# A two-block decoder kernel: key weights of the second memory attention taken out of the weight ring, four of its eight key tiles computed in four earlier openings

## The reference, cut to what matters

```python
def second_block(x, mem, ...):
    mem_n = rms_norm_2(mem, mem_norm)                 # 256 memory tokens, once for both layers
    for i in range(2):
        g = ln_gains[i]
        hn = rms_norm_2(x, g[0])
        t = rglru_mixer(hn, ...) if i == 0 else rwkv7_mixer(hn, ...)
        x = x + rms_norm_2(t, g[1])
        c = mem_cross_attention(rms_norm_2(x, g[2]), mem_n, c_w_q[i], c_w_kv[i], c_w_o[i])
        x = x + rms_norm_2(c, g[3])
        m = sqrelu_mlp(rms_norm_2(x, g[4]), m_w_up[i], m_w_down[i])
        x = x + rms_norm_2(m, g[5])
```

## Time and profile before

| | |
|---|---|
| median of 3 runs | 3470.85 us (3470.57 to 3474.96) |
| the profiled execution's own time | 3472.6 us |
| span in the profile | 3470.8 us |
| mean granted TensorE clock | 0.999 |
| PE busy | 3429.4 us, 99% of the span |
| PEld, DVE, ACT, POOL busy | 77%, 48%, 41%, 40% |
| DMA | 317.43 MB, mean 91 GB/s |
| L1053, products of memory keys | 256 records, 56.5 us |
| L593, fillers | 72 records, 34.7 us |

### The profile page before, as it was taken

The page is one execution under the profiler, slowest core; times in us unless marked ns, Lnnn a source line. Parts: engine busy times, 40 slices in busy tenths (PEclk is TensorE's granted clock), DMA queues, the critical chain, the costliest instruction groups (busy, mean ns, idle before and its releaser), DMA issues.

```text
span 3470.8 us, 52494 instructions
## 1 busy us (share of the span) xinstructions
PE 3429.4 (99%) x19196; PEld 2686.1 (77%) x19196; DVE 1652.4 (48%) x2657; ACT 1416.0 (41%) x2843; POOL 1387.3 (40%) x1112
## 2 busy tenths in 40 slices
PE   9999999999999999999999999999999999999999
PEld 7877787888788777888887777788874677868887
DVE  2565666442335765764424643412257874433032
ACT  3245534332333554343325643533317244444232
POOL 4632244444455223544444152444410222424444
PEclk9999999999999999999999999999999999999999
DMA  4421122222224111222232331222233221213222
GB/s 146 126 86 55 55 79 97 97 97 100 99 96 136 55 55 64 95 91 97 97 103 100 107 103 61 92 97 97 97 133 98 86 64 57 97 55 109 97 97 85
DMA packets 105274, 317.43 MB, mean 91 GB/s; under 512 B 27008, under 2 KB 31232, under 8 KB 104192
## 3 DMA queue, kind: packets, MB, share of 16 engines
q1 hardware_dynamic: 93168, 301.00, 25.8%
q10 hardware_dynamic: 11920, 13.85, 1.5%
HBM read 304.32 MB, written 7.34 MB: 90 GB/s over the span
## 4 chain that ended last, share of the span: by engine, by line
PE 91%; DVE 4%; ACT 1%; DMA 1%; DVEq 1%; issue 1%; SPq 0%; POOL 0%; ACTq 0%; POOLq 0%
PE ps L586 24%; PE ps L588 23%; PE ps L587 23%; PE ps L1338 2%; PE ps L1053 2%; PE ps L775 2%; PE ps L627 1%; PE ps L622 1%; PE ps L795 1%; DMA ring<-in_weights 1%; PE ps L820 1%; PE ps L623 1%; PE ps L1123 1%; PE ps L1157 1%; PE ps L1284 1%
## 5 line engine op out<-in xcount | busy, mean ns | idle before, releaser
L3302 POOL TENSOR_TENSOR ring_r<-ring,rounded_r 128x512 fp32r<-128x512 f32 x505 | 666.9, 1321 | 1803.6 <-ACT rounded_r L1617 1795.2
L586 PE MATMUL ps<-source_hi,rounded_r 128*128 128x512 f32 x2360 | 935.7, 396 | 3.9 <-DVE Y_lo L3237 1.9
L587 PE MATMUL ps<-source_hi,ring_r 128*128 128x512 f32 x2360 | 919.0, 389 | 0.0
L1617 ACT ACTIVATE rounded_r<-ring 128x512 fp32r<-128x512 f32 x512 | 323.1, 631 | 1306.2 <-PE ps L588 1142.8
L3304 POOL TENSOR_TENSOR ring_r<-ring,rounded_r 128x512 fp32r<-128x512 f32 x505 | 704.2, 1394 | 0.0
L588 PE MATMUL ps<-X_lo,rounded_r 128*128 128x512 f32 x1456 | 568.1, 390 | 0.0
L586 PEld LDWEIGHTS ps<-source_hi,rounded_r 128*128 128x128 f32 x2360 | 443.3, 188 | 104.8 <-issue 11.0
L587 PEld LDWEIGHTS ps<-source_hi,ring_r 128*128 128x128 f32 x2360 | 443.6, 188 | 89.1 <-issue 1.9
L588 PEld LDWEIGHTS ps<-X_lo,rounded_r 128*128 128x128 f32 x1456 | 273.2, 188 | 58.0
L1618 ACT ACTIVATE rounded_r<-ring 128x512 fp32r<-128x512 f32 x512 | 316.3, 618 | 0.0
L588 PE MATMUL ps<-N_lo,rounded_r 128*128 128x512 f32 x760 | 296.0, 389 | 0.0
(11 more groups left out here) (534 smaller groups left out, 5509.7 us busy)
## 6 DMA issues: line engine op xcount, KB each, us to landing
ring<-in_weights SPq DMA_DIRECT2D x556, 512.0 KB, 3.3
X<-in_x SPq DMA_DIRECT2D x4, 512.0 KB, 6.8
PAIR<-Z ACTq DMA_DIRECT2D x32, 64.0 KB
residual<-X ACTq DMA_DIRECT2D x1, 2048.0 KB, 9.4
X<-residual SPq DMA_DIRECT2D x1, 2048.0 KB, 9.1
ring<-in_weights SPq DMA_DIRECT2D x16, 128.0 KB, 2.6
SWAP<-Z ACTq DMA_DIRECT2D x4, 256.0 KB, 6.0
MEM<-in_mem ACTq DMA_DIRECT2D x1, 1024.0 KB, 4.9
```

What stands on the lines that cost most here:

```text
L586: mm(o, lh, rh, start=start, stop=False)
L587: mm(o, ll, rh, start=False, stop=False)
L1617: av(RH[:, j, FRONT], ring[:, j, FRONT], ACT.Copy).then_inc(w_hi_half, 1)
L3302: nc.gpsimd.tensor_tensor(RL[:, j, FRONT], ring[:, j, FRONT], RH[:, j, FRONT].bitcast(F32), ALU.subtract).then_inc(w_lo_half, 1)
```

## The change

- The weights of layer 1's memory keys leave `weights` and become an input of their own, `keys`. Two DMAs on ACT's queue bring them into `MIXED` (`KEYS_W`), four tiles each, 2 MB: the first right behind the load of the memory at the start of the second block, the second in the second half of the MLP of `tail(0)`, behind its `up`.
- Key tiles 0 to 3 (`HELD` = 4) are computed ahead of four openings: tile 0 ahead of `lru_out`, in place of `warm(3, 3)`; tile 1 ahead of the queries, in place of `warm(0, 2)`; tile 2 ahead of the product with the values, in place of `warm(4, 2)`; tile 3 around the norm ahead of the MLP, four matmuls ahead of its sums, two ahead of its spread, two behind it, in place of `warm(1, 1)` and `warm(3, 3)`, with `warm(4, 2)` after them.
- ACT copies each of these tiles out of its bank (`key_held`) into the place of its weights. TensorE waits for these copies ahead of lane 3 of two first quads, ahead of the output product, and behind the first quad of `up`. DVE scales the four at the start of its second half of the MLP, and ACT saves them to `D3`.
- Tile 4 takes the place of the first of the eight behind the last `down`. Tiles 5 to 7 follow, and the sums of squares of the norm ahead of RWKV are spread among them: squares 0 and 1, 2 and 3, then 4 to 7.

```diff
-B_RWKV = B_K1 + C_MK
+B_RWKV = B_K1
...
+            def next_keys(c, bank, first=0, end=KT):
+
+                pe.wait_ge(keys_in, KEYS_LANDED + c // HELD * 16 + 16)
+                half = c % 2 if c >= HELD else 0
+                for k in range(first, end):
+                    ins = mm(ps[:, bank, half * S2:half * S2 + S2], KEYS_W[:, c % HELD, k * P:k * P + P], MN[:, k, :], start=(k == 0), stop=(k == KT - 1))
+                if end == KT:
+                    ins.then_inc(keys_made, 1)
...
-                warm(0, 2)
+                if l == 0:
+                    next_keys(1, HELD_BANK[1])
+                else:
+                    warm(0, 2)
...
-                warm(4, 2)
+                if l == 0:
+                    next_keys(2, HELD_BANK[2])
+                else:
+                    warm(4, 2)
...
+                if l == 0:
+                    pe.wait_ge(keys_held, HELD_AT + 3)
                 gemm(B + B_MO, C_MO, AH, YL, t_ready, l * 32 + 8, SRC[f"o{l}"], 4)
+                if l == 0:
+                    next_keys(3, HELD_BANK[3], 0, 4)
                 rms_out(4 + 6 * l)
-                warm(1, 1)
+                if l == 0:
+                    next_keys(3, HELD_BANK[3], 4, 6)
+                else:
+                    warm(1, 1)
                 rms_spread(4 + 6 * l)
-                warm(3, 3)
+                if l == 0:
+                    next_keys(3, HELD_BANK[3], 6)
+                    warm(4, 2)
+                else:
+                    warm(3, 3)
...
                 if l == 0:
-                    mem_keys(B_K1, 0, K1_BANKS[0], lambda: rms_out(6))
+                    next_keys(4, K1_BANKS[0], 0, 4)
+                    rms_out(6)
+                    next_keys(4, K1_BANKS[0], 4)
                     rms_spread(6)
                     return
...
-            warm(3, 3)
-            gemm(B_LRU_OUT, C_LRU_OUT, AH, ZL2[:, 16:24, :], t_ready, 0, SRC["lru_out"], skewed=True)
+            next_keys(0, HELD_BANK[0])
+            gemm(B_LRU_OUT, C_LRU_OUT, AH, ZL2[:, 16:24, :], t_ready, 0, SRC["lru_out"], skewed=True, held=1)
...
+            next_keys(5, K1_BANKS[0], 0, 6)
+            sums_in(0, 2)
+            next_keys(5, K1_BANKS[0], 6)
+            next_keys(6, K1_BANKS[1], 0, 4)
+            sums_in(2, 4)
+            next_keys(6, K1_BANKS[1], 4)
+            next_keys(7, K1_BANKS[1], 0, 2)
+            sums_in(4, KT)
+            next_keys(7, K1_BANKS[1], 2, 5)
+            rms_spread(7)
+            next_keys(7, K1_BANKS[1], 5)
...
+                        if l == 0:
+                            act.wait_ge(keys_scaled, SCALED_AT + 1)
+                            act.dma_start(D3[:, 0:HELD, :], KEYS_HELD).then_inc(keys_saved, 16)
                         with act.Fori(0, C_HUP // RING) as i:
...
+                        if l == 0:
+                            act.wait_ge(keys_saved, KEYS_LANDED + 16)
+                            act.dma_start(KEYS_W, a["keys"][:, HELD:KT, :]).then_inc(keys_in, 16)
...
             act.dma_start(MN, a["mem"]).then_inc(mem_in, 16)
+            act.dma_start(KEYS_W, a["keys"][:, 0:HELD, :]).then_inc(keys_in, 16)
+
+            def key_held(c):
+                act.wait_ge(keys_made, MADE + c + 1)
+                av(KEYS_HELD[:, c, :], ps[:, HELD_BANK[c], 0:S2], ACT.Copy).then_inc(keys_held, 1)
...
+                    if (l, h) == (0, 1):
+                        dve.wait_ge(keys_held, HELD_AT + HELD)
+                        tt(KEYS_HELD, KEYS_HELD, MEM_FACTOR.unsqueeze(1).to_broadcast([P, HELD, S2]), ALU.mult).then_inc(keys_scaled, 1)
```

More of the change, by code:

```diff
@@ L641, in high_first, with first_quad @@
                     product(split + j, j, bank + j, hi, lo)
-            def first_quad(split, bank, hi, lo, ready, base, step=1, banks_free=None, lanes=RING - 1, before=None, skewed=False, late=None):
+            def first_quad(split, bank, hi, lo, ready, base, step=1, banks_free=None, lanes=RING - 1, before=None, skewed=False, late=None, held=0):
                 def step_of(k, j):
@@ L1045, in mem_squares, with mem_keys, gemm @@
                 ins.then_inc(rms_var, 1)
-            def mem_keys(first, c, bank, halfway=None):
+            def next_keys(c, bank, first=0, end=KT):
[5 more added lines that the diff above has]
+                    ins.then_inc(keys_made, 1)
+            def mem_keys(first, c, bank):
                 arrived((first + c) // RING, c % RING)
                 for k in range(KT):
-                    if k == KT // 2 and halfway is not None:
-                        halfway()
                     ins = mm(ps[:, bank, (c % 2) * S2:(c % 2) * S2 + S2], w(c % RING, k), MN[:, k, :], start=(k == 0), stop=(k == KT - 1))
                 ins.then_inc(used, 1)
-            def gemm(first, tiles, hi, lo, free, base, src, bank=0, event=None, before=None, skewed=False, second=None, third=None, lanes=RING - 1, late=None, lag=1):
+            def gemm(first, tiles, hi, lo, free, base, src, bank=0, event=None, before=None, skewed=False, second=None, third=None, lanes=RING - 1, late=None, lag=1, held=0):
                 done = 0
@@ L1060, in gemm @@
                     if skewed:
-                        first_quad(n_split(first), bank, hi, lo, src_lo, src, 1, (free, base), lanes, before, skewed, late)
+                        first_quad(n_split(first), bank, hi, lo, src_lo, src, 1, (free, base), lanes, before, skewed, late, held)
                     else:
@@ L2150, in _ @@
             last_slot(LRU_OUT_QUAD)
+            key_held(0)
             out_tiles(B_LRU_OUT, 2, gain(0, 1), bias="b_out")
@@ L2956, in mem_low, with mem_keys @@
                 remainder(MNL, MN, MNHF, mem_lo)
-            def mem_keys(first, dst, bank):
-                for i in range(C_MK // 2):
-                    dve.wait_ge(used, first + 2 * i + 2)
+            def mem_keys(made, first, dst, bank):
+                for i in range(len(bank)):
+                    dve.wait_ge(made, first + 2 * i + 2)
                     tt(dst[:, 2 * i:2 * i + 2, :], ps[:, bank[i], :].rearrange("p (k s) -> p k s", k=2),
@@ L3467, in second_weights @@
     gate = i["a_gate_w_2"][0].reshape(2, 2, 2, 2, P, 2, P).transpose(1, 0, 4, 2, 5, 3, 6).reshape(4, P, CHUNK)
-    keys = [lin(i["c_w_kv_2"][l][:, :D]) for l in range(2)]
-    out = [lin(i["a_w_in_2"][0]), gate, keys[0], lin(i["a_w_out_2"][0]), *tail(0), keys[1]]
+    out = [lin(i["a_w_in_2"][0]), gate, lin(i["c_w_kv_2"][0][:, :D]), lin(i["a_w_out_2"][0]), *tail(0)]
     key = lin(i["b_w_rkv_2"][0][1])
```

50 lines of the change are left out of this document (34 added, 16 removed).

## The result

| | before | after |
|---|---|---|
| median | 3471.21 us (20 runs, 3468.76 to 3474.96) | 3477.98 us (20 runs, 3472.66 to 3485.51) |
| the profiled execution's own time, and its span | 3472.6, 3470.8 us | 3477.6, 3475.8 us |
| mean granted TensorE clock | 0.999 | 0.997 (0.996 to 0.999 over the runs) |

The ratio is **1.0016**, 95% interval 1.001 to 1.0022: the change makes the kernel 6.8 us slower, 3.5 to 7.6. 3471.9 with a range of 3467.0 to 3476.5 was forecast, and no change held to be likely: wrong on both.

What follows compares the result with a forecast made beforehand. TensorE, with 91% of what ended last, was taken to bound the kernel. The terms 0.9 + 1.0 + 1.5 + 1.2 - 6.6 + 3.0 = +1.0 us gave 3471.9 us, range 3467.0 to 3476.5.

Steps and rivals of the forecast that it cites:

- Opening 0: Ahead of `lru_out`: a key tile (3.46 us) replaces fillers (2.58), so the opening grows by 0.9 us.
- opening 1: Ahead of the queries: +1.7 us for a tile replacing two fillers, less waits that go in the quad behind, net +1.0.
- opening 3: Ahead of the MLP: half a tile ahead of the norm's sums makes root, reciprocal, spread and residual 1.2 us later.
- Opening 2: Ahead of the attention output: the tile ends 1.5 us after the next product's old start; ACT's copy costs nothing.
- The keys start at 2575.5 instead of 2582.11: -6.6, out of 13.9: Ahead of RWKV: with four tiles gone another chain sets the end, TensorE idles 3.4 us, and 6.6 us are gained.
- Rival (b): The stretch ahead of RWKV keeps all that was moved out: 4.6 - 13.9 = -9.3, 3461.6 us; chance 0.04.
- Loads ... I take +3.0: Opening of `lru_in`: first 2 MB load delays the ring's chunk; +3.0 us, between 0 and +4.1 (the load goes first).
- Rival (a): At `lru_in` the ring isn't delayed, or a little: -2.0 us, 3468.9; chance 0.22.
- Rival (c), "The clock falls": TensorE's clock halves in the 3.4 us gap ahead of RWKV's keys: +1.8 us, 3473.7; chance 0.13.
- Against it: 3.4 is short of 3.7: Ahead of RWKV: the 3.4 us gap is shorter than the 3.7 us before the clock fell at the kernel's end.
- It turns to over 0.2% slower only if the clock stays down 12 us: Clock fall ahead of RWKV: (6.9 - 1.0) / 0.5 gives 12 us at half clock, 3478 and up; chance 0.05.
- Rival (d): A copy or bank wait priced at nothing stands on the path, ACT stopped in `key_held`: 6 us, 3478; chance 0.06.

Runs made afterwards that it cites:

- e8: The change with the first load issued later and three key tiles held, tile 3 back in the stretch ahead of RWKV; 3466.16 against 3470.97 us, ratio 0.9988.
- e1: The change with the first 2 MB key load issued at the ninth chunk of `lru_in`, not at its opening; 3471.25 against 3471.46 us, ratio 1.0001.
- e4: The kernel before plus only the 2 MB load at the opening of `lru_in`, nobody computing with it; 3478.97 against 3471.46 us, ratio 1.0022.
- e7: The change with the first load as four loads of 4 KB rows, issued behind the first chunk of `lru_in`; 3471.60 against 3470.97 us, ratio 1.0002.
- e9: The change with four fillers in the stall at `lru_in` and three ahead of the RWKV keys; 3472.99 against 3470.72 us, ratio 1.0011.
- e3: The change with the first 2 MB load as four loads of 4 KB rows at the same place; 3477.10 against 3471.46 us, ratio 1.0016.
- e5: The change with four fillers in the stall ahead of the second quad of `lru_in`; 3474.08 against 3470.97 us, ratio 1.0009.
- e6: The change with the first load, in 16 KB rows, issued behind the first chunk of `lru_in`; 3480.96 against 3470.97 us, ratio 1.0026.

## Why the prediction was wrong

- *Opening 0, +0.9; opening 1, "Net +1.0"; opening 3, +1.2*: right (0.91, 1.03, 1.2).
- *Opening 2, "+1.5"*: right at the place, but net +0.75. The term stopped at the tile's end and didn't follow it into the output product, as was done for opening 1 and its quad. What that product gave back was not tried by itself.
- *"The keys start at 2575.5 instead of 2582.11: -6.6, out of 13.9"*: right, -6.45, with all four pauses where they were put (1.1, 1.2, 1.2 and 3.4 forecast; 0.88, 0.60, 1.12 and 3.30 measured). That most of the moved work brings nothing, because DVE and ACT set the pace, is confirmed by e8 from the other side. Rival (b) falls. Its 3461.6 had also left out the ring's +3.0: 4.6 - 13.9 + 3.0 = -6.3 is not more than 0.2%.
- *"Loads ... I take +3.0"*: **the term that was mis-sized.** The mechanism was right: no slack, the load nearly first, TensorE waiting for POOL. The bounds were 0 to +4.1, and +5.0 was measured. The upper end let the chunk run at full speed from 1872.5 on; in fact the ring's first packets moved from 1870.9 on, but the chunk then took 4.9 us to reach ACT and not 2.4, and was 0.9 later than that bound. No row of before could show two queues together. The value was put below the end, though the text itself held that the code's row sizes put it "near the top". Rival (a) falls with it, and e1 and e4 show term and cause.
- *Rival (c), "The clock falls"*: **the step that failed, and the larger error**: the sum puts the clock at nothing, for a chance of 0.13, and looks for a fall at the RWKV gap only, though the sum had just made a new stall of 3 us at `lru_in`, where TensorE goes from dense to nothing. A forecast stall is itself a gap for the clock to fall in. At both places it fell in the profile, for 2.4 and 3.1 us, not 1.8 once. "Against it: 3.4 is short of 3.7" took the one fall in the trace of before for a bound; e7 shows a fall behind 1.84 us. The Trainium skill ("TensorE: Matmul & The Clock Gate", Why this matters for your kernels) warns of gaps over about 3 us between bursts. It was cited, with "by it this rival would be the likelier case", and its chance was still left low. The falls behind 4.78 and 3.30 us agree with the warning; the one behind 1.84 us shows that a shorter pause was not safe here.
- *"It turns to over 0.2% slower only if the clock stays down 12 us"*: the two falls last 6.8 us each, 11 us of both on dense products, and with the ring's term larger by 2 the time passed that mark.
- *Rival (d)*: nothing of it in the timelines.

With the ring's term at 5.0, opening 2 at 0.75 and two falls of the clock (5.5) the sum would have been +7.9 at the first RWKV products, where the trace, which starts the block 0.25 earlier, has +7.7; its span ends at +5.0, and the medians are 6.8 apart. With the ring's term alone put right it would have been 3.9 - 6.45 + 5.0 = +2.5, 3473.3, inside the range; e9, with most of the clock's share out, measured +2.3. So it is the clock that took the time out of the range. (The range's own terms add up to 3476.7 at its upper end, not 3476.5.)

## What to carry to other kernels

A large load that isn't needed for long is not free where a ring restarts with no slack: look for the moment at which the first chunk behind it is waited for, take the bound "the load goes first" (here even that was 0.9 us short), or issue it later: eight chunks later cost nothing here. Whoever forecasts a new stall of a dense TensorE should price a fall of its clock in the same line. And work moved out of a stretch gains only up to the next chain there; what idle time is left over is room to move some of it back, here one tile of four. The later load took the loss away (e1, 3471.25 against 3471.46), and with that tile back in the stretch the kernel was 3 to 5 us faster than before.

## What was not expected of the hardware

- **The clock fell behind pauses of very different lengths, and behind the same pause not always.** The gap of 3.30 us ahead of RWKV's keys is the same in six profiles; the clock fell in it in three (the change, e3, e7), not in e5 and e6, and in e1 it had fallen 9 us ahead of the keys, behind waits of 0.60 and 1.12 us among the squares. In e7 it fell 0.9 us after a pause of 1.84 us had ended:

```profile
1872.00:1874.00 2.00, 0.21 (x1) 0.21 (x2) 0.00 (x0) 2.00 (x3) 1.53 (x2) 1.00 1.01 360
1874.00:1875.00 1.00, 1.00 (x5) 0.77 (x5) 0.00 (x0) 0.71 (x1) 0.98 (x1) 0.84 1.01 410
1875.00:1878.00 3.00, 3.00 (x9) 2.33 (x8) 0.00 (x0) 2.12 (x5) 1.42 (x2) 0.50 1.02 416
```

  The columns are those of the first stretches above. TensorE is busy all through the last two rows and still at half. Inside the long stalls of `lru_in` the fall came 2.6 us after TensorE's last product in e3, 3.0 in the change, 3.2 in e4 and 5.3 in e6. The clock then stayed at half for 6.8 us in the change, e3 and e4, and for 3.4 in e6 and e7, as in the falls among the squares of e1 and e9.
- **The falls go with the scatter of the times.** The change's 20 runs lie 12.9 us apart, those of before 6.2. Its three runs with a mean granted clock of 0.999 took 3472.7 to 3474.1 us, the eight with 0.998 3473.9 to 3478.8, the nine with 0.997 or 0.996 3476.8 to 3485.5.
- **A queue that starts behind a load under way starts late**, beyond the turns: first packets 3.6 us after SP's request in the change and 3.4 in e3, 1.0 without the load. With a load asked for at nearly the same time as the ring's chunk it was still 2.7 us (e6) and 2.0 (e7).
